# A hybrid decoder layer on one core: first up panels walked among adaLN groups, and squared tiles summed on VectorE

## The reference

```python
mod = silu(c) @ w_ada + b_ada                     # adaLN: 2048 x 18432, nine vectors
sh1, sc1, gt1, shm, scm, gtm, sh2, sc2, gt2 = split(mod, 9)
h = h + 0.5 * gt1 * swiglu(rmsnorm(h, n1) * (1 + sc1) + sh1, w_up1, w_down1)   # d_ff 5632
h = h + gtm * (mixer(rmsnorm(h, nm) * (1 + scm) + shm) @ w_out)
h = h + 0.5 * gt2 * swiglu(rmsnorm(h, n2) * (1 + sc2) + sh2, w_up2, w_down2)
y = rmsnorm(h, n_final)
```

## Time and profile before

| | |
|---|---|
| three timed runs | median 2850.51 us (2848.46 to 2855.27) |
| profiled execution | 2847.77 us, its span 2845.8 us |
| mean granted TensorE clock | 0.986 |
| TensorE matmul / weight load busy | 97% / 90% of the span |
| VectorE / ScalarE / GpSimd busy | 49% / 37% / 1% |
| HBM traffic | 605 MB, mean 213 GB/s |
| chain that ended last | TensorE 89%, DMA 4%, VectorE 3%, ScalarE 3%, issue 1% |

### The profile page before, as it was taken

One profiled execution on the slowest core, in us unless ns is written; L12 is line 12 of the kernel. 1 busy time (PEld: TensorE's weight loads), 2 busy tenths in 40 slices (PEclk: granted clock), 3 DMA queues, 4 the chain that ended last, 5 costly groups with the idle time before them and its releaser, 6 DMA issues.

```text
span 2845.8 us, 51903 instructions
## 1 busy us (share of the span) xinstructions
PE 2753.5 (97%) x21861; PEld 2551.9 (90%) x21861; DVE 1388.1 (49%) x1714; ACT 1049.2 (37%) x1066; POOL 29.7 (1%) x64
## 2 busy tenths in 40 slices
PE   5799999999999999999999999999999999999998
PEld 2499989999999898899987999989799999999997
DVE  0444445444444665656546555464544445444454
ACT  1333333333334432534333444343433333333332
POOL 0000000000000000000001000000000000000000
PEclk9799999999999999999999999999999999999999
DMA  9766665666665677423356566666665445555453
GB/s 382 282 245 233 251 224 182 222 250 229 235 230 169 241 282 281 167 104 105 118 209 221 212 231 232 240 256 230 244 245 232 177 157 183 194 182 182 151 173 122
DMA packets 93649, 605.11 MB, mean 213 GB/s; under 512 B 10560, under 2 KB 10688, under 8 KB 35152
## 3 DMA queue, kind: packets, MB, share of 16 engines
q1 hardware_dynamic: 88720, 582.06, 55.6%
q0 software_dynamic: 4368, 19.94, 2.0%
q10 hardware_dynamic: 432, 1.21, 0.1%
HBM read 590.55 MB, written 12.62 MB: 212 GB/s over the span
## 4 chain that ended last, share of the span: by engine, by line
PE 89%; DMA 4%; DVE 3%; ACT 3%; issue 1%; DVEq 0%; ACTq 0%; SPq 0%
PE acc L1780 24%; PE acc L1781 23%; PE acc L1788 23%; PE mp L1853 4%; PE acc L2010 2%; PE acc L2011 2%; PE acc L2016 2%; ACT whi L754 2%; DMA raw<-in_ada 2%; DVE wlo L1159 1%; DMA raw<-in_win 1%; DMA raw<-in_up 1%; PE mp L2084 1%; PE mp L2076 1%; PE mp L1880 1%
## 5 line engine op out<-in xcount | busy, mean ns | idle before, releaser
L1159 DVE TENSOR_TENSOR wlo<-raw,whi 128x2048 fp32r<-128x2048 f32 (+2 forms) x445 | 929.8, 2090 | 847.9 <-ACT whi L754 847.7
L1780 PE MATMUL acc<-xhi,whi 128*128 128x264 f32 x4064 | 1024.0, 289 | 7.1 <-ACT whi L754 7.1
L1781 PE MATMUL acc<-xlo,whi 128*128 128x264 f32 x4064 | 1008.8, 286 | 0.0
L754 ACT ACTIVATE whi<-raw 128x2048 fp32r<-128x2048 f32 (+2 forms) x445 | 777.7, 1748 | 573.2 <-PE acc L1788 401.0
L1780 PEld LDWEIGHTS acc<-xhi,whi 128*128 128x128 f32 x4064 | 769.7, 189 | 85.1 <-issue 77.8
L1781 PEld LDWEIGHTS acc<-xlo,whi 128*128 128x128 f32 x4064 | 771.0, 190 | 0.3
L1788 PE MATMUL acc<-xhi,wlo 128*128 128x264 f32 x4064 | 531.8, 284 | 0.0
L1788 PEld LDWEIGHTS acc<-xhi,wlo 128*128 128x128 f32 x4064 | 506.4, 188 | 0.0
L1780 PE MATMUL acc<-uhi,whi 128*128 128x264 f32 x1408 | 355.2, 289 | 5.0 <-DVE ulo L1293 5.0
L1781 PE MATMUL acc<-ulo,whi 128*128 128x264 f32 x1408 | 348.9, 284 | 0.0
L1780 PEld LDWEIGHTS acc<-uhi,whi 128*128 128x128 f32 x1408 | 265.8, 189 | 6.6 <-DVE ulo L1293 5.6
(11 more groups left out here) (332 smaller groups left out, 1872.6 us busy)
## 6 DMA issues: line engine op xcount, KB each, us to landing
raw<-in_up SPq DMA_DIRECT2D x176, 1024.0 KB, 4.9
raw<-in_ada SPq DMA_DIRECT2D x144, 1024.0 KB, 6.5
raw<-in_down SPq DMA_DIRECT2D x128, 704.0 KB, 4.1
raw<-in_win SPq DMA_DIRECT2D x69, 1024.0 KB, 6.5
raw<-in_wgate SPq DMA_DIRECT2D x32, 1024.0 KB, 4.8
raw<-in_wout SPq DMA_DIRECT2D x16, 1024.0 KB, 5.9
raw<-in_wproj SPq DMA_DIRECT2D x24, 512.0 KB, 4.8
raw<-in_cache SPq DMA_DIRECT2D x12, 1024.0 KB, 5.3
```

What stands on the lines that cost most here:

```text
L754: act.activation(whi[:, s.slot(SPLIT), 0:width], raw[:, r.slot(RAW), 0:width], ACT.Copy)\
L1159: v.tensor_tensor(wlo[:, s.slot(SPLIT), 0:width], raw[:, r.slot(RAW), 0:width], whi[:, s.slot(SPLIT), 0:width].bitcast(F32), ALU.subtract)\
L1780: mm(dst, w, xh, start=starts and k == 0, stop=False)
L1781: mm(dst, w, xl, start=False, stop=False)
```

## The change

- `LATE` takes the place of `MIXED` in the last body of both FF1 halves and in four QKV rounds: weight panel 2 moves ahead of the second adaLN panel, so that three adaLN panels lie between panels 2 and 3.
- The opening: SP loads the first two up panels after 24 adaLN panels (`G_X` = 6 groups) rather than after 32. ScalarE and VectorE split them after `norm_group(1)`. TensorE walks them in pieces: two tiles after each adaLN panel of group 6, two after each of the second and third panel of group 7, and the last four tiles after fold 7. Each piece waits for its tiles of the norm.
- Norms 1 and 2 (`walked`): two adaLN panels, tiles 0 to 4, one adaLN panel, tiles 5 to 9, one adaLN panel, tiles 10 to 15, fold. ScalarE copies the rows after its last tile.
- Squares: VectorE adds each squared tile into `sacc` or `sacco` (`add_square`, after two memsets in `clear_squares`), one tile behind; TensorE sums the accumulated tile and the sixteenth square, which isn't added, in two matmuls at the end (`total_squares`). Tile sums on TensorE are gone, except for the first norm's, which stay.
- The first down half-panel waits for 11 of the 22 hidden tiles; the second waits for all.
- con is loaded in parts: the identity, the ones and the selector by ScalarE's queue as before (`small_loaded` now counts to 48), the masks by GpSimd's queue after the first norm (`masks_loaded`, waited for by VectorE and TensorE in the mixer). TensorE waits for `small_loaded` only ahead of fold 0.

The diff, cut to its core (new tiles and semaphores, the same waits at other places and unchanged lines are left out):

```diff
@@ -122,10 +122,10 @@
-MIXED = (0, 1, None, None, 2, None, None, 3)
+LATE = (0, 1, None, 2, None, None, None, 3)
...
-FF1_PLAN = ((WIDE, 5), (MIXED, 1))
-QKV_PLAN = ((WIDE, 1), (MIXED, 4))
+FF1_PLAN = ((WIDE, 5), (LATE, 1))
+QKV_PLAN = ((WIDE, 1), (LATE, 4))
@@ -153,6 +153,8 @@
+G_X = 6
+R_X = 4 * G_X
...
@@ -210,6 +211,11 @@
     for body, rounds in plan:
...
+def r_first(k):
+    return k if k < R_X else k + 2
...
@@ -604,7 +614,7 @@
             for k in range(RAW):
...
-            with sp.Fori(1, ADA_FIRST // RAW) as i:
+            with sp.Fori(1, G_X) as i:
@@ -613,10 +623,10 @@
                     if early is not None and k < 2:
-                        load(At(r0 - 4 + k), w[w0 + x])
+                        load(At(r0 - 4 * len(early) + k), w[w0 + x])
                         if k == 1:
-                            for q in range(4):
-                                load(At(r0 - 2 + q), t["ada"][4 * early + q])
+                            for q in range(4 * len(early)):
+                                load(At(r0 - 4 * len(early) + 2 + q), t["ada"][4 * early[0] + q])
@@ -641,8 +651,9 @@
             for o in range(2):
-                ffn(R_FF1 + o * R_FF1_HALF, t["up1"], t["down1"], o, FF1_PLAN, G_FIRST + o * G_FF1_HALF)
-            bodies(QKV_PLAN, R_QKV + 4, t["win"], 0, G_QKV, G_N1)
+                ffn(R_FF1 + o * R_FF1_HALF, t["up1"], t["down1"], o, FF1_PLAN, G_FIRST + o * G_FF1_HALF,
+                    None if o else range(G_X, G_FIRST))
+            bodies(QKV_PLAN, R_QKV + 4, t["win"], 0, G_QKV, (G_N1,))
...
@@ -703,6 +714,8 @@
+            pool.wait_ge(x_lo, N_FIRST)
+            pool.dma_start(con[:, C_INCL:C_SEL], t["con"][:, C_INCL:C_SEL]).then_inc(masks_loaded, 16)
@@ -799,10 +812,10 @@
-            def tile_square(buf, q0, t0, q, i, stride=4):
+            def tile_square(buf, n, t0, q, i, stride=4):
...
-                act.wait_ge(square_summed, seq(q0 + q - 1, stride, i).val())
+                act.wait_ge(square_added, seq((KD + 2) * n + 2 + q, stride, i).val())
@@ -816,11 +829,10 @@
                 for k in range(KD):
-                    if k == 1:
-                        copy_rows(At(g), At(r + 3))
...
+                copy_rows(At(g), At(r + 3))
...
@@ -858,36 +870,37 @@
                         if o and k % 2:
-                            tile_square(sq, q0, t0, k // 2, i)
+                            tile_square(sq, nq, t0, k // 2, i)
...
                         if k % 2:
-                            tile_square(sq, q0, t0, k // 2, 3)
+                            tile_square(sq, nq, t0, k // 2, 3)
                 if o:
-                    root(q0 + KD)
+                    root(KD + 2 * nq + 2)
...
-            act.dma_start(con[:, :], t["con"]).then_inc(small_loaded, 16)
+            act.dma_start(con[:, 0:C_INCL], t["con"][:, 0:C_INCL]).then_inc(small_loaded, 16)
+            act.dma_start(con[:, C_SEL:CONST_W], t["con"][:, C_SEL:CONST_W]).then_inc(small_loaded, 16)
...
                 if g == G_SQ:
...
-                    act.wait_ge(small_loaded, 32)
+                    act.wait_ge(small_loaded, 48)
...
                 if g == G_SCALE:
...
-                copy_rows(At(g) if g else None, At(4 * g + 3))
-                if g == G_FIRST - 1:
-                    split_hi(At(S_FF1), R_FF1 - S_FF1, first=True)
+                copy_rows(At(g) if g else None, At(r_first(4 * g + 3)))
                 if g >= G_SCALE:
...
-            split_hi(At(S_FF1 + 1), R_FF1 - S_FF1, first=True)
+                if g == G_X - 1:
+                    for k in range(SPLIT):
+                        split_hi(At(S_FF1 + k), R_X, first=True)
...
@@ -1272,6 +1285,17 @@
+            def clear_squares(buf, total):
+                v.memset(buf[:, 1, :], 0.0).then_inc(square_added, 1)
+                v.memset(total[:, :], 0.0).then_inc(square_added, 1)
+            def add_square(buf, total, n, q, i, stride=4):
+                dve.wait_ge(square_ready, seq(KD * (n + 1) + q, stride, i).val())
+                dve.wait_ge(square_added, seq((KD + 2) * n + q + 2, stride, i).val())
+                b = (q + 1) % 2
+                v.tensor_tensor(total[:, :], total[:, :], buf[:, b, :], ALU.add).then_inc(square_added, 1)
@@ -1302,10 +1326,15 @@
+                if o:
+                    clear_squares(sq, sacc)
...
                             if k:
+                                if o:
+                                    add_square(sq, sacc, 2 if n else 0, q, i)
@@ -1326,8 +1355,9 @@
                 if g >= G_SCALE:
...
-            for k in range(SPLIT):
-                split_lo(At(S_FF1 + k), R_FF1 - S_FF1)
+                if g == G_X - 1:
+                    for k in range(SPLIT):
+                        split_lo(At(S_FF1 + k), R_X)
...
@@ -1735,11 +1766,13 @@
             for k in range(2):
...
+            clear_squares(sqo, sacco)
...
                     for k in range(per):
+                        add_square(sqo, sacco, 1, k, i, per)
@@ -1790,14 +1823,14 @@
-            def duo(s, r0, a, made, ready):
-                for j in range(2):
+            def duo(s, r0, a, made, ready, ks):
+                for j in range(2 if ks[0] == 0 else 0):
...
-                for k in range(KD):
+                for k in ks:
@@ -1874,84 +1907,95 @@
-            def tile_sum(buf, q0, q, i, first=False, last=False, stride=4):
-                pe.wait_ge(square_ready, seq(q0 + q + 1, stride, i).val())
-                mm(mp[:, 0, 0:NT], ones, buf[:, q % 2, :], start=first, stop=last).then_inc(square_summed, 1)
-            def panels(body, s0, r0, a0, g0, i, ready=None, r_first=None, behind=None):
+            def total_squares(buf, total, n):
+                pe.wait_ge(square_added, (KD + 2) * (n + 1))
+                mm(mp[:, 0, 0:NT], ones, total[:, :], start=True, stop=False).then_inc(square_summed, 1)
+                pe.wait_ge(square_ready, KD * (n + 2))
+                mm(mp[:, 0, 0:NT], ones, buf[:, 1, :], start=False, stop=True).then_inc(square_summed, 1)
+            def panels(body, s0, r0, a0, g0, i, begun=None):
...
                 for k, x in enumerate(body):
-                    if ready and x == 0:
-                        duo(At(s0), At(r_first), At(a0), x_lo, ready)
+                    if begun and x == 0:
+                        begun()
...
-                    elif not (ready and x == 1):
+                    elif not (begun and x == 1):
...
-                    if behind and x is not None:
-                        behind(x, i)
                 if p:
...
-            def early(g, r):
-                for m in range(4):
-                    ada(m, At(g), At(r + m))
-                def behind(x, i):
-                    if isinstance(i, int) and x == 1:
-                        fold(At(g))
-                return behind
-            def ffn(n, o, s0, r0, a0, plan, g0, ready=None, r_first=None, behind=None):
+            def walked(s0, a0, r, ready, g):
+                def begun():
+                    for m in range(2):
+                        ada(m, At(g), At(r + 2 + m))
+                    duo(At(s0), At(r), At(a0), x_lo, ready, range(0, 5))
+                    ada(2, At(g), At(r + 4))
+                    duo(At(s0), At(r), At(a0), x_lo, ready, range(5, 10))
+                    ada(3, At(g), At(r + 5))
+                    duo(At(s0), At(r), At(a0), x_lo, ready, range(10, KD))
+                    fold(At(g))
+                return begun
+            def ffn(n, o, s0, r0, a0, plan, g0, begun=None):
                 for body, rounds, p, r, g in stretches(plan):
...
-                    if ready and p == 0:
-                        panels(body, s0, r0, a0, g0, 0, ready, r_first, behind)
+                    if begun and p == 0:
+                        panels(body, s0, r0, a0, g0, 0, begun)
...
                     with pe.Fori(first, rounds) as i:
...
-                pe.wait_ge(hidden_lo, (2 * n + o + 1) * HALF)
+                pe.wait_ge(hidden_lo, (2 * n + o) * HALF + DOWN)
...
-                q0 = N_SQ + KD if n else KD
-                def down(i, first=False):
+                def down(i):
                     for q in range(4):
...
-                        if o and not (first and q == 0):
-                            tile_sum(sq, q0, q - 1, i, first=first and q == 1)
+                        if q == 0:
+                            pe.wait_ge(hidden_lo, (2 * n + o + 1) * HALF)
...
-                down(0, True)
-                with pe.Fori(1, 4) as i:
+                with pe.Fori(0, 4) as i:
...
                 if o:
-                    tile_sum(sq, q0, 3, 3, last=True)
+                    total_squares(sq, sacc, 2 if n else 0)
+            def first_ready(k):
+                return NB * (k // 4) + k % 4 + 2
...
             for g in range(G_FIRST):
...
-                if g == 0:
-                    pe.wait_ge(small_loaded, 32)
                 for p in range(4):
-                    ada(p, turn_no, At(4 * g + p))
```

(22 more changed lines are left out.)

22 lines of the change are left out of this document (12 added, 10 removed).

## The result

| | kernel before | changed kernel |
|---|---|---|
| median | 2850.98 us (2848.46 to 2855.27, four runs) | 2814.07 us (2812.85 to 2815.49, four runs) |
| ratio to before | | 0.9869, 95% interval 0.9852 to 0.9886 |
| profiled execution, its span | 2847.77, 2845.8 us | 2814.42, 2812.6 us |
| mean granted TensorE clock | 0.986 | 0.989 |

The change saves 36.9 us between the medians and 33.4 us between the profiled executions; 40.4 were forecast. The predicted 2809 us is 5 us too low, inside its range of 2801 to 2824.

What follows compares the result with a forecast made beforehand. The prediction took TensorE as the bound everywhere after the opening, and the DMA queue in the opening. Its terms, 8.3 + 19.4 + 5.0 + 5.0 + 2.7 = 40.4 us, gave 2809 us, range 2801 to 2824.

Steps and rivals of the forecast that it cites:

- Part 1: Opening, to the end of the walked pair: earlier start and pair walked inside groups 6 and 7, 8.3 us saved.
- (a): Opening: TensorE starts without con and par, and masks leave the front; queue 4.2 us ahead.
- (b): Opening: first up pair walked inside groups 6 and 7; held slots let the queue run dry, adaLN panels some 4.5 us later.
- t: Opening: the moment group 5's last adaLN panel is done, 78.1 us, from which the walk's times were counted.
- R1: Rival: the opening stays at half clock, a loss of 5 us in place of 8.3 saved; 2823 us, chance 0.12.
- R2: Rival: splits no stall, queue stays fed, LATE and norm 2 give all; 46.6 us saved, 2804 us, chance 0.15.
- Part 2: Squares in two down norms and the out stage: 44 sums leave TensorE's path, VectorE's adds hidden, 19.4 us saved.
- R4: Rival: VectorE paces squared tiles, slower once an add and its waits exceed 2.1 us; at 2.5, 2870 us; chance 0.03.
- Part 3: Hidden tiles: the four waits ahead of the first down panels go, 5.0 us saved, bounds 3.5 to 5.
- Part 4: LATE for MIXED in FF1's last bodies and QKV: panel 3 late by only 0 to 0.2, 5.0 us saved.
- Part 5: Walks of norms 1 and 2: norm 1's VectorE-bound, ending 1.7 us earlier; norm 2's TensorE-bound, 1.0 saved; sum 2.7 us.
- R3: Rival: LATE only moves the wait, panel 3 as late as before; 5 us less saved, 2815 us, chance 0.15.

Runs made afterwards that it cites:

- e7: Changed kernel with the first up pair split ahead of norm group 1 instead of behind it: 2807.49 us.
- e10: Changed kernel with an unused 2112-column VectorE add ahead of each square's add in both FFs' o=1 down stages: 2815.90 us.
- e5: Changed kernel with MIXED back in place of LATE: 2816.54 us.
- e1: Kernel before with only the squares' change: squares added on VectorE, two sums on TensorE at each norm's end: 2834.31 us.
- e8: Changed kernel with three adaLN panels ahead of the walks of norms 1 and 2 and one inside, instead of two and two: 2811.75 us.
- e11: Changed kernel with the edits of e7 and e8 together: 2808.14 us.
- e4: Changed kernel with the first up pair loaded and split after all 32 adaLN panels and walked in one piece: 2817.52 us.
- e3: Kernel before with only the opening's earlier start: con in parts, wait at fold 0, masks on GpSimd's queue, no panel moved: 2844.28 us.
- e6: Changed kernel with the body (0, 1, None, 2, None, 3, None, None) in place of LATE, so panel 3 lies between adaLN panels: 2810.44 us.
- e9: The changed kernel measured and profiled again, unchanged: 2814.64 us.
- e2: Kernel before with only the hidden tiles' change: the first down half-panel waits for 11 hidden tiles: 2843.16 us.

## Why the prediction was right, and where it wasn't

**Part 1 was right in its mechanism**, its size in part by luck. (a) gave 4.95 us (4.2 forecast), (b) 4.3 (4.1), and the queue ran dry where and because the forecast said. But t itself came 5.9 us earlier, not 4.2, and the walk then took 1.1 us longer than counted, since behind the wait of 2.61 us the clock fell to half for most of its last four tiles: two misses of which one takes back most of the other. And the same opening gained 6.5 to 9.5 us in six executions, so against them (b) is worth 2.0 to 5.0. R1 didn't come: behind the burst's start at half clock the clock was 1.00 from 90 to 110 us. R2, a queue that stays fed, didn't either, but e7 shows what it would have been worth in the opening: 4.9 us, where R2 had 3.7.

**Part 2 was right**: 19.5 us for 19.4, in the ledger of every kernel that had it (19.1 to 19.5). The reason given for its being hidden was wrong: the 0.8 us of idle time ahead of take_sublayer isn't what protects it. e10 used more than that up and the tile's pitch didn't move. With it falls the sentence that without that cover each add would cost 0.43 us. R4's threshold of 2.1 us falls as well: 0.43 + 2.35 = 2.8 us of added work a tile is 1.6 us more than the 1.65 - 0.44 = 1.2 us that the forecast counted as cover, so by its account each of the 32 tiles should have become 1.6 us longer, and none did.

**Part 3 was sized too small**, 5.0 for 7.3 us. The step took the waits out of the list of waits and stopped there. One of them stood ahead of a stretch at half clock, worth 1.5 us; the other 0.8 us over the four places lie beyond the waits that the list has, and weren't taken apart. That 5 was also the upper bound had no reason behind it.

**Part 4 failed**: 5.0 us forecast, -3.1 in the ledger, and MIXED loses as much (e5). The step that failed is "late by 0 to 0.2". It set a path of 6.48 + 0.7 + 1.9 = 9.1 us against a need after 9.0. Measured, the path is 0.68 + 6.76 + 1.92 and the handing over between them, 9.51 us in all (1056.34 to the matmul that waited, at 1065.85), and the need comes after 8.69. The path is 0.4 longer than counted. The forecast's 0.7 us stands for the 0.68 by which the load, behind the adaLN load in SP's in-order queue, goes out later; but the landing took 0.28 us more besides, and the steps between landing, split and matmul (0.15 us) had no term. The need is 0.3 earlier, since adaLN panels in a row take 0.86 us and not 1.06. The same account would have made MIXED late by 6.48 + 1.9 - 5.85 - 2.1 = 0.4 us where the earlier trace rows show 0.85 (its path, from 1041.74 to the matmul at 1050.44, was 8.70 us, with 0.3 us of such steps): held against the kernel before it would have shown its own error. In place of the 0.85 us a round that LATE was to save, the three later rounds gained 0.06 us in all. The loss of 3.1 us lies elsewhere: 1.2 in QKV's first round, and in FF1's first half 0.4 of longer wait and some 1.5 of the clock that fell behind it.

That settles the three later QKV rounds. It doesn't settle the first one, nor FF1's first half: there LATE and MIXED alike wait 2.0 to 2.4 us in the kernels with the whole change, and in QKV that round had waited 0.85 before, 1.3 in e1. The landing was longer there, 8.0 to 8.1 us in the changed kernel, e7, e8 and e11 against 6.76 in the changed kernel's next round:

```profile
1026.56 7.99 DMA raw<-in_win
```

So it isn't chance, but what lengthens it is open. One packet of an engine's instruction fetch fell into this landing in the changed kernel and in e4, e5 and e7 to e11 (7.9 to 8.1 us), and none into that of the same round in the kernel before and in e1 to e3 (6.5 to 7.0 us), nor into the changed kernel's short one. But in e3's third round a landing of 7.65 us and a wait of 2.0 us had none. No experiment took it apart.

**Part 5 was half right**: 1.1 us for 2.7. Norm 2 gained 1.3 for 1.0 (between 0.0 and 1.3 in the other kernels with this walk). Norm 1 was to gain 1.7 and lost 0.2. The step "the walk is VectorE's" failed: after only two adaLN panels TensorE stands still for 4.1 us and begins at half clock, so that the walk became TensorE's (6 matmuls x 0.22 = 1.32 us a tile, where VectorE needs 0.92), as the forecast had said of norm 2 alone. e8 put a third panel ahead of the walk, the wait fell to 2.8, and the gain came out at 1.97. In e6 and e7 the walk also began at full clock, after 2.5 and 2.8 us, because the clock had fallen earlier, behind the waits for the squares, and the two adaLN panels took 3.4 and 3.3 us instead of 1.92. It fell again 0.5 and 1.2 us into the walk, and the gain was 0.6 and 0.5. TensorE in e7:

```profile
941.92 0.71 PE L1915 MATMUL mp<-sq,con 128*128 128x264 f32 x2 [0.94 <-ACT sq L820]
942.57 3.28 PE L1886 MATMUL mp<-raw,csl 128*32 128x512 f32 x16
948.61 0.36 PE L1838 MATMUL acc<-xhi,whi 128*128 128x264 f32 x1 [2.76 <-DVE xlo L1267]
```

**The sum** was off by 6.8 us against the ledger: Part 4 by -8.1, Part 5 by -1.6, Part 3 by +2.3, the rest by +0.6. The medians show only 3.5 us of this (36.9 for 40.4), since the profiled execution of before lay 3.2 us under its median. R3 was the case that came true; it priced 2815 and was given 0.15.

## What to carry to other kernels

A load that is moved ahead may go out behind another one in its queue: before counting a wait as saved, work out the path from the slot's release to the landing, by an account that first gives the wait which the old kernel shows. When two panels are held in the slots of an in-order queue, let them be split before anything else that the splitting engines have to do, since the queue stands still until they are (4.9 us here, in the ledger). An engine beside the bound has to be done within the period of a tile; the idle time in front of one of its instructions is not the room that it has.

## What the runs showed of the hardware

The granted clock of TensorE after a wait doesn't follow from the wait's length alone. After 1.76 us it fell, after 1.77 us at the like place of the same execution it didn't; at panel 3 in FF1's first half it fell after 2.23 us (the changed kernel), 2.12 (e5), 2.28 (e8), 2.04 (e9) and 2.15 (e10 and e11), and not after 2.07 (e4) or 2.37 (e7, whose stretch behind that wait is shown). Waits of 0.66 and 0.94 us at the end of FF1's down stage left it up in e8; in e6 and e7 it fell 0.4 and 1.1 us behind the second of them.

```profile
387.00:389.00 2.00, 2.00 (x18) 2.00 (x18) 2.00 (x2) 0.49 (x2) 0.00 (x0) 1.00 0.92 360
```

A fall costs about 1.5 us (FF1's first half lost 1.89 us with a wait 0.40 longer; in e2 two like waits gave 3.55 and 2.02). After 4.1 us or more without work, the first matmuls ran at 1.2 GHz in each walk quoted here. In the changed opening the clock was at half at 84 to 88 us, behind 4.59 us of idle time, and at full from 90 to 110, where TensorE waited 0.75 and 0.72 us and then 2.61, behind which the clock was at half again. In the last 5 us of this stretch it was busy for 1.84, still at full clock:

```profile
105.00:110.00 5.00, 1.84 (x16) 0.97 (x8) 2.15 (x9) 1.81 (x4) 0.00 (x0) 1.00 0.99 398
```

The Trainium skill (TensorE: Matmul & The Clock Gate, the section on HAM oscillation) says that bursts parted by DMA waits can each start throttled. The stretches at 84 and 110 us agree, although what ended those waits was VectorE's work; the waits of 2.07 and 2.37 us in FF1, behind which the clock stayed full, show that it need not happen.

The landing of a 1 MB panel by the same queue took 6.48 us before and 6.76 and 7.99 us after in like rounds of QKV, and that decided whether TensorE waited 0.8 or 2 us.
